# A YOCO conformer trunk on one core: the last expert pair kept on chip, a layer norm root in halves, output weights in four parts

## The reference, cut to what matters

```python
def conformer_conv(h, w_in, b_in, w_dw, b_dw, ln_g, ln_b, w_out, b_out):
    a, gate = jnp.split(h @ w_in + b_in, 2, axis=-1)
    u = a * jax.nn.sigmoid(gate)
    u = lax.conv_general_dilated(u, w_dw[:, None, :], ...) + b_dw
    u = jax.nn.silu(layer_norm(u, ln_g, ln_b))
    return u @ w_out + b_out

def hierarchical_moe(h, r_grp, r_exp, w_gate, w_up, w_down):
    ...
    hid = jax.nn.silu(a) * u * gates[:, :, None]
    y = jnp.einsum("tef,efd->td", hid, w_down)

x = x + conformer_conv(rms_norm(x, a_norm), ...)
x = x + hierarchical_moe(rms_norm(x, ffn_norm[0]), ...)
kv = shared_kv(x, kv_norm, w_kv)
x = x + dilated_attention(rms_norm(x, b_norm), ..., kv)
x = x + hierarchical_moe(rms_norm(x, ffn_norm[1]), ...)
out = rms_norm(x, final_norm)
```

## Time and profile before

| | |
|---|---|
| median of 3 runs | 1626.92 us (1626.81 to 1626.94) |
| the profiled execution's own time | 1628.82 us |
| its span, first to last instruction | 1627.0 us |
| mean granted clock of PE | 0.966 of full speed |
| busy: PE / DVE / ACT / POOL | 1517.0 / 1052.5 / 672.4 / 388.2 us |
| chain that ended last | PE 74%, DVE 12%, DMA 9%, ACT 3% of the span |

### The profile page before, as it was taken

How to read it: one execution, slowest core, us unless ns; L and a number is a source line. 1 busy time by engine, 2 the same in 40 slices (tenths; PEclk the granted TensorE clock), 3 DMA queues, 4 the chain that set the end, 5 groups by cost and what they waited for, 6 DMA issues and landing times.

```text
span 1627.0 us, 19661 instructions
## 1 busy us (share of the span) xinstructions
PE 1517.0 (93%) x7236; PEld 1172.2 (72%) x7236; DVE 1052.5 (65%) x1284; ACT 672.4 (41%) x730; POOL 388.2 (24%) x341
## 2 busy tenths in 40 slices
PE   6999798999999967999999999999999799999992
PEld 5887485766666735888888888888888576766661
DVE  6995728555656529775857777686872865555554
ACT  5111635455555515324233232423243555555542
POOL 3000012222222214332405142240501222222120
PEclk9999798999999987999999999999999899999996
DMA  5223507788888836212112121211336468888854
GB/s 204 78 74 117 219 39 286 306 339 339 338 344 341 332 125 231 83 54 75 64 52 90 39 83 59 77 60 56 120 148 239 173 282 356 347 360 340 346 233 168
DMA packets 52358, 309.83 MB, mean 190 GB/s; under 512 B 10336, under 2 KB 16096, under 8 KB 38496
## 3 DMA queue, kind: packets, MB, share of 16 engines
q1 hardware_dynamic: 41808, 291.28, 45.6%
q0 software_dynamic: 9648, 16.80, 2.9%
q10 hardware_dynamic: 864, 1.26, 0.2%
HBM read 299.33 MB, written 28.31 MB: 201 GB/s over the span
## 4 chain that ended last, share of the span: by engine, by line
PE 74%; DVE 12%; DMA 9%; ACT 3%; issue 2%; SPq 0%; DVEq 0%; POOL 0%; ACTq 0%; POOLq 0%
PE PS L1774 11%; PE PS L1837 5%; PE PS L1839 5%; PE PS L1838 5%; DMA WR<-w_up 5%; DVE taps_sb L1104 4%; PE PS L1922 3%; PE PS L1938 3%; PE PS L1753 3%; PE PS L1749 3%; PE PS L1750 3%; PE PS L1736 3%; PE PS L1734 3%; PE PS L1735 3%; PE PS L1853 3%; PE PS L1855 3%
## 5 line engine op out<-in xcount | busy, mean ns | idle before, releaser
L1375 DVE TENSOR_TENSOR wgl<-WR,wgh 128x2048 fp32r<-128x2048 f32 x66 | 148.6, 2290 | 213.9 <-ACT wgh L882 212.8
L728 POOL TENSOR_TENSOR KQ<-rope_ab 64x512 f32<-64x512 f32 x96 | 173.7, 1809 | 364.7 <-DVE rope_ab L1464 361.1
L1774 PE MATMUL PS<-WR,SC 128*128 128x512 f32 x528 | 234.9, 598 | 3.1 <-ACT SC L919 1.7
L1774 PEld LDWEIGHTS PS<-WR,SC 128*128 128x128 f32 x528 | 99.4, 191 | 118.3 <-issue 116.2
L951 ACT ACTIVATE wh<-wraw 128x1024 fp32r<-128x1024 f32 x76 | 80.3, 1057 | 249.5 <-PE PS L1839 248.7
L1375 DVE TENSOR_TENSOR wul<-WR,wuh 128x2048 fp32r<-128x2048 f32 x66 | 148.0, 2284 | 0.9 <-ACT wuh L882 0.9
L882 ACT ACTIVATE wgh<-WR 128x2048 fp32r<-128x2048 f32 x66 | 122.4, 1905 | 60.1 <-DMA WR<-w_gate 60.1
L882 ACT ACTIVATE wuh<-WR 128x2048 fp32r<-128x2048 f32 x66 | 122.6, 1905 | 31.1 <-PE PS L1736 19.5
L1464 DVE TENSOR_TENSOR rope_ab<-PS,rope_sb 32x512 f32<-32x512 f32 x192 | 131.9, 687 | 2.6
L1749 PE MATMUL PS<-wgh,xgh 128*128 128x512 f32 x264 | 110.8, 420 | 2.5 <-DVE wgl L1375 2.5
L1446 DVE TENSOR_TENSOR wl<-wraw,wh 128x1024 fp32r<-128x1024 f32 x76 | 93.1, 1225 | 28.0 <-ACT wh L951 26.3
(11 more groups left out here) (286 smaller groups left out, 3284.4 us busy)
## 6 DMA issues: line engine op xcount, KB each, us to landing
WR<-w_gate SPq DMA_DIRECT2D x33, 2048.0 KB, 15.5
WR<-w_up SPq DMA_DIRECT2D x33, 2048.0 KB, 16.7
WR<-w_down SPq DMA_DIRECT2D x33, 2048.0 KB, 9.0
wraw<-w_qkv SPq DMA_DIRECT2D x72, 512.0 KB, 3.3
WR<-w_in SPq DMA_DIRECT2D x8, 1024.0 KB, 4.9
WO<-w_out SPq DMA_DIRECT2D x2, 2048.0 KB, 8.0
xn_dram<-SC SPq DMA_DIRECT2D x8, 512.0 KB, 2.9
HT<-y_dram SPq DMA_DIRECT2D x8, 512.0 KB, 6.6
```

The source lines that it names most:

```text
L728: nc.gpsimd.tensor_tensor(to, cos, sin, ALU.add).then_inc(rope_done, 1)
L1375: V.tensor_tensor(lo[:, kts, :], raw[:, kts, :], hi[:, kts, :].bitcast(F32), ALU.subtract).then_inc(done, 1)
L1774: ins = M.matmul(PS[3 + h][:, :], hidT[:, ft, :], wd[b][:, ft, h * 512:(h + 1) * 512], start=ft == 0, stop=ft == FT - 1)
```

## The change

1. **Start.** ACT's `y_done` copies, and the wait for the constants ahead of them, go behind the four roots.
2. **Taps.** DVE takes 3 taps of chunk 0 before `gated(1)` instead of 9, and the others after it.
3. **Output weights.** `w_out` comes in four transfers of 1 MB, at other places of SP's queue, each further forward.
4. **Mean.** DVE adds chunks 0 to 5 up ahead; PE multiplies that sum, chunk 6, and, by 16 products of 128x128 with a matrix `onesp`, chunk 7 as it lies in phases in `yph[0]`, before its way through DRAM.
5. **Root.** ACT reads the variance from PSUM with EPS as bias; root, reciprocal, the first product, silu and rounding of chunk 0 go in two halves of the tokens; the tables of Sqrt and Silu are loaded ahead by dummy operations; PE starts chunk 0 with its 16 hi products, the 8 lo ones follow. `wo_lead` 5 to 7 go between the silu of chunks 1 to 3.
6. **Last pair.** Its rows are not scattered. POOL stores zeros to their places in `y_dram` at the start of the layer (`clear`), SP loads `y_dram` while the last pair is computed, and DVE adds these rows (`add_stored`, the eight operations of `combined`) then. DVE builds a 128 x 512 matrix of mixing weights for each block of the last pair (`place_last`), PE transposes it, and PE sums its rows (`sum_rows`: 8 products of 512 columns for each expert) straight into PSUM; DVE adds them to X (`add_last`).
7. **Around it.** The hidden tile of the last pair is copied by ACT, not DVE. PE transposes the rows of "kv" once all four quarters of X are there. SP issues the first loads of `w_qkv` before the last pair ends, and `rope` after the stores of `x_dram`.

```diff
 out_of_phases(1)
 win_load(7)
+sp.dma_start(WE, a["w_out"][:, 0:2, :]).then_inc(wout_in[0], 16)
 out_of_phases(3)
+sp.dma_start(WO[:, 6:KT, :], a["w_out"][:, 6:KT, :]).then_inc(wout_in[1], 16)
 into_phases(5)
 into_phases(6)
 out_of_phases(5)
 into_phases(7)
 sp.wait_ge(u_mm, KT)
-sp.wait_ge(taps_done, len(BY_TAPS))
-sp.dma_start(WO[:, 0:KT // 2, :], a["w_out"][:, 0:KT // 2, :]).then_inc(wout_in[0], 16)
+sp.dma_start(WO[:, 2:4, :], a["w_out"][:, 2:4, :]).then_inc(wout_in[0], 16)
 out_of_phases(6)
 out_of_phases(7)
-sp.wait_ge(conv_in[0], (len(BY_BANDS) + 1) // 2 * PH * 16)
-sp.dma_start(WO[:, KT // 2:, :], a["w_out"][:, KT // 2:, :]).then_inc(wout_in[1], 16)
+sp.wait_ge(taps_done, len(BY_TAPS))
+sp.dma_start(WO[:, 4:6, :], a["w_out"][:, 4:6, :]).then_inc(wout_in[1], 16)
...
-    sp.wait_ge(y_stored[l][0], (last + 1) * 16)
-    sp.wait_ge(y_stored[l][1], seconds)
+    for b in range(2):
+        sp.wait_ge(y_stored[l][b], last * 16)
+    sp.wait_ge(y_cleared.sem, y_cleared.at(32 * (l + 1)))
     for n in range(NT):
+        if n == 2:
+            sp.wait_ge(gate_mm[l], 2 * last + two + 1)
         for k in range(2):
-            sp.dma_start(yg[k][:, n, :], y_dram[l][k * T + n * P:k * T + (n + 1) * P, :]).then_inc(x_in[n], 16)
...
+last_0 = moe_sp(0)
+sp.wait_ge(up_mm[0], 2 * last_0 + 1)
...
+    def clear(b):
+        nc.gpsimd.tensor_copy(zcol[b], slot_ids[:, bass.ds(2 * last + b, 1)]).then_inc(p_steps, 1)
+        steps.n += 1
+        steps.wait()
+        nc.gpsimd.tensor_tensor(idle[:, :], ident[:, 0:1], ident[:, 0:1], ALU.mult)
+        pool.indirect_dma_start(y_dram[l], bass.IndirectOffsetOnAxis(ap=zcol[b], axis=0), zeros, None,
+                                bounds_check=2 * T - 1, oob_is_err=False).then_inc(y_cleared.sem, 16)
...
+    for b in range(2):
+        clear(b)
-    scatter(0, last)
-    with pool.If(two > 0):
-        scatter(1, last)
...
+        act.wait_ge(const_in, 48)
+        for c, s in enumerate(y_done):
+            nc.scalar.activation(spare[:, 4 + c:5 + c], ident[:, 0:1], ACT.Copy).then_inc(s, 1)
...
+nc.scalar.activation(spare[:, 13:14], eps, ACT.Sqrt)
...
 wo_lead(4)
-wo_lead(5)
-act.wait_ge(ln_d, KT + 1)
-nc.scalar.activation(lnstd, lnstd, ACT.Sqrt).then_inc(ln_sq, 1)
-wo_lead(6)
-wo_lead(7)
-for c in range(KT):
-    act.wait_ge(ln_n, c + 1)
-    nc.scalar.activation(SL[:, c, :].rearrange("p (t s) -> p s t", s=PH), HTQ[:, c, :].rearrange("p (s t) -> p s t", s=PH),
+act.wait_ge(var_mm, KT)
+for ts in HALVES:
+    nc.scalar.activation(turned(lnstd)[:, :, ts], turned(PS[5][:, :])[:, :, ts], ACT.Sqrt, bias=eps).then_inc(ln_sq, 1)
+nc.scalar.activation(spare[:, 14:15], eps, ACT.Silu)
+def silu(c, m, ts):
+    act.wait_ge(ln_n, m)
+    nc.scalar.activation(in_phases(SL[:, c, :])[:, :, ts], turned(HTQ[:, c, :])[:, :, ts],
                          ACT.Silu, bias=cv[:, C_LNB + c:C_LNB + c + 1],
                          scale=cv[:, C_LNG + c:C_LNG + c + 1]).then_inc(silu_done, 1)
+    act.wait_ge(silu_done, m)
+    nc.scalar.activation(HTh[:, c, tok], SL[:, c, tok], ACT.Copy).then_inc(silu_lead, 1)
+for m, ts in enumerate(HALVES):
+    silu(0, m + 1, ts)
+for c in range(1, KT):
+    silu(c, c + 2, slice(0, TP))
+    if c < 4:
+        wo_lead(4 + c)
...
+            def copy_hidT(b):
+                act.wait_ge(hT_mm[l], 2 * i + (b + 1))
+                if b == 1:
+                    act.wait_ge(down_mm[l], 2 * i + 1)
+                nc.scalar.activation(hidT.rearrange("p a b -> p (a b)"), PS[2][:, :], ACT.Copy).then_inc(hidT_done[l], 1)
             with act.If(two > 0):
                 gate_lead(1, i + 1, 2 * i + 1)
                 up_lead(1, i + 1, 2 * i + 1)
                 silu_gate(1)
+            copy_hidT(0)
+            act.wait_ge(spread_mm.sem, spread_mm.at(l + 1))
+            nc.scalar.activation(spread_w[0], PS[5][:, :], ACT.Copy).then_inc(spread_sb.sem, 1)
             store_y(0)
             with act.If(two > 0):
+                copy_hidT(1)
+                act.wait_ge(y_done[l], 2 * i + 2)
+                nc.scalar.activation(yst[1], yst[0], ACT.Copy)
+                nc.scalar.activation(spread_w[1], PS[5][:, :], ACT.Copy).then_inc(hidT_done[l], 1)
+                act.wait_ge(hidT_done[l], 2 * i + 3)
+                nc.scalar.activation(spread_w[0], PS[6][:, :], ACT.Copy)
                 store_y(1)
...
-taps(0, 0, 9)
+taps(0, 0, 3)
 gated(1)
-taps(0, 9, 12)
+taps(0, 3, 12)
...
 biased(6)
+for b in range(2):
+    dve.wait_ge(conv_in[b], (2 - b) * PH * 16)
+steps.mark(V.tensor_tensor(lnstd, HTQ[:, 0, :], HTQ[:, 1, :], ALU.add))
+for c in range(2, 6):
+    steps.wait()
+    steps.mark(V.tensor_tensor(lnstd, lnstd, HTQ[:, c, :], ALU.add))
+presum_done.append(steps.n)
 biased(7)
 dve.wait_ge(mean_mm, 1)
-for b in range(2):
-    dve.wait_ge(conv_in[b], (len(BY_BANDS) + 1 - b) // 2 * PH * 16)
 for c in range(KT):
+    if c >= KT - 2:
+        dve.wait_ge(conv_in[KT - 1 - c], (2 + (c == KT - 1)) * PH * 16)
...
     wo_trail(c)
-dve.wait_ge(var_mm, KT)
-V.tensor_scalar(lnstd, PS[5][:, :], EPS, None, ALU.add).then_inc(ln_d, 1)
-dve.wait_ge(ln_sq, KT + 1)
-steps.step(V.reciprocal(lnstd, lnstd))
+wol_done.append(steps.n)
 dve.wait_ge(ln_d, KT)
-for c in range(KT + 2):
+for m, ts in enumerate(HALVES):
+    root, first = turned(lnstd)[:, :, ts], turned(HTQ[:, 0, :])[:, :, ts]
+    dve.wait_ge(ln_sq, KT + m + 1)
+    steps.step(V.reciprocal(root, root))
+    V.tensor_tensor(first, first, root, ALU.mult).then_inc(ln_n, 1)
+for c in range(1, KT + 2):
     if c < KT:
         V.tensor_tensor(HTQ[:, c, :], HTQ[:, c, :], lnstd, ALU.mult).then_inc(ln_n, 1)
     if c >= 2:
         if c - 2 >= KT // 2:
             wo_trail(c - 2)
-        dve.wait_ge(silu_lead, c - 1)
+        dve.wait_ge(silu_lead, c)
         V.tensor_tensor(HTl[:, c - 2, :], SL[:, c - 2, :], HTh[:, c - 2, :].bitcast(F32), ALU.subtract).then_inc(silu_trail, 1)
...
-def combined(n, l):
+def add_stored(n, l):
     dve.wait_ge(x_in[n], 48 * (l + 1))
-    steps.step(V.scalar_tensor_tensor(X[:, n, :], yg[0][:, n, :], wt[0][:, n, :], X[:, n, :], ALU.mult, ALU.add))
-    V.scalar_tensor_tensor(X[:, n, :], yg[1][:, n, :], wt[1][:, n, :], X[:, n, :], ALU.mult, ALU.add).then_inc(x_upd.sem, 1)
+    steps.step(V.scalar_tensor_tensor(X[:, n, :], yq[n][0], wt[0][:, n, :], X[:, n, :], ALU.mult, ALU.add))
+    V.scalar_tensor_tensor(X[:, n, :], yq[n][1], wt[1][:, n, :], X[:, n, :], ALU.mult, ALU.add).then_inc(y_added.sem, 1)
+def add_sum(n, h):
+    cols = slice(h * 512, (h + 1) * 512)
+    return V.tensor_tensor(X[:, n, cols], X[:, n, cols], PS[SUM_BANKS[(2 * n + h) % 4]][:, :], ALU.add)
+def add_last(n, l, two):
+    if n == 0:
+        dve.wait_ge(sum_add[l].sem, 2 * NT * two + sum_add[l].at(0))
+    for h in range(2):
+        dve.wait_ge(sum_mm[l].sem, 2 * NT * two + sum_mm[l].at(2 * n + h + 1))
+        ins = add_sum(n, h)
+    ins.then_inc(x_upd.sem, 1)
...
+        steps.step(V.scalar_tensor_tensor(mix[b], col, last2[:, b:b + 1], wt_all, ALU.is_equal, ALU.mult))
+        steps.mark(V.tensor_tensor(to, rk_hot[:, 0:NT, :], over_rows(mix[b][:, 0:NT]), ALU.mult))
+        steps.step(V.tensor_tensor(part, rk_hot[:, NT:, :], over_rows(mix[b][:, NT:]), ALU.mult))
+        if b == 0:
+            steps.step(V.tensor_tensor(to, to, part, ALU.add))
+        else:
+            V.tensor_tensor(to, to, part, ALU.add).then_inc(spread_set.sem, 1)
...
+            steps.wait()
+            for b in range(2):
+                place_last(b)
-            copy_hidT(0)
+                hidden(1)
+            for n in range(NT):
+                add_stored(n, l)
+            dve.wait_ge(y_added.sem, y_added.at((l + 1) * NT))
             with dve.If(two > 0):
-                hidden(1)
-                copy_hidT(1)
+                for n in range(NT):
+                    for h in range(2):
+                        dve.wait_ge(sum_mm[l].sem, sum_mm[l].at(2 * n + h + 1))
+                        add_sum(n, h).then_inc(sum_add[l].sem, 1)
...
+    if k == "kv":
+        pe.wait_ge(x_upd.sem, x_upd.at(k, NT))
...
+    if l == 0:
+        for n in range(NT):
+            pe.wait_ge(silu_lead, n // 2 + 1)
+            if n == 0:
+                pe.wait_ge(v_steps, wol_done[0])
+            for h in range(2):
+                hi, _ = rows(0, slice(n * P, (n + 1) * P))
+                wh_c, wl_c = weights(0, slice(h * 512, (h + 1) * 512))
+                M.matmul(PS[2 * n + h][:, :], hi, wh_c, start=True, stop=False)
+                M.matmul(PS[2 * n + h][:, :], hi, wl_c, start=False, stop=False)
+        tile_ready(0)
+        for n in range(NT):
+            for h in range(2):
+                _, lo = rows(0, slice(n * P, (n + 1) * P))
+                wh_c, _ = weights(0, slice(h * 512, (h + 1) * 512))
+                ins = M.matmul(PS[2 * n + h][:, :], lo, wh_c, start=False, stop=False)
+        row_used(ins)
+    for c in range(0 if l else 1, half):
...
-order = (0, 1, 2, 3, 5, 4, 6, 7)
-for c in order:
-    if c in BY_TAPS:
```

(37 more changed lines are left out.)

84 lines of the change are left out of this document (57 added, 27 removed).

## The result

The changed kernel takes 1598.51 us (median of 4 runs, 1596.6 to 1601.56) against 1626.93 (4 runs, 1626.81 to 1628.97): 28.4 us less, a ratio of 0.9818 with a 95% interval of 0.9807 to 0.983. Run again in another call it took 1595.70 (5 runs, 1594.42 to 1597.4) against 1627.83, 32.1 less, 0.9807 (0.9793 to 0.9822). All nine runs together have a median of 1597.04; 1597 was forecast, with a range of 1590 to 1608. Within one call its runs span 3 to 5 us, those of before 2 to 6, so it does not scatter more.

What follows compares the result with a forecast made beforehand. PE is busy for 93% of the span, so only its waits can gain or lose: 1.2 - 1.7 + 6.5 + 2.5 + 5.9 + 11.3 + 4.3 = 30.0 off 1626.9 gives 1597 us, range 1590 to 1608.

Steps and rivals of the forecast that it cites:

- Start: Kernel start: ACT's squares no longer wait for constants, copies start 1.7 us earlier, 0.5 goes back at gated(1); gain 1.2 us.
- Output weights: Convolution 5: the WO[6:8] load queued ahead of u_dram(5) makes u land late; loss 1.7 us, bounds 0 and 2.9.
- Mean: Layer norm: centring starts 5.5 us after convolution 7 instead of 12.05; gain 6.5 us, bounds 5.0 and 6.7.
- Rival D: Centring still waits for chunk 7 from DRAM and the halves run one after the other: 1606 us; chance 0.06.
- Variance: Layer norm: PE, busy with the mean right ahead, takes 9.3 us instead of 11.8 from centring; gain 2.5 us.
- Root and first chunk: Variance to end of the projection's first chunk: halves and hi products first take 10.5 us instead of 16.4; gain 5.9.
- B: Low-clock rival: PE's new short bursts stay at the low level in variance, first chunk, sums and turns: 1608 us; chance 0.18.
- Layer 0's end: After down in layer 0: PSUM sums replace scatter, load and add, turned rows copied at 613.1, not 624.39; gain 11.3 us.
- Layer 1's end: After the last down in layer 1: both experts' sums and last scaling finish earlier; gain 4.3 us, bounds 3 and 5.3.
- Nothing: place_last, zero rows and POOL's clear lie in idle time or beside loops where PE has its weights; no cost.
- C: Transfers in the way: zero rows or earlier weights push first gate weights by 2.5 us a layer: 1602 us; chance 0.10.
- E: Slower: sums wait for the adds and PE stays at the low level, 2.6 us a product: 1638 us; chance 0.04.

Runs made afterwards that it cites:

- wout_old: Changed kernel, but w_out comes in two 2 MB transfers at their old queue places, the mean staying new; 1602.92 us.
- mean_old: Changed kernel, but PE sums the eight chunks one by one as they return from DRAM, as before; 1600.01 us.
- pair_old: Changed kernel, but with parts 6 and 7 taken back: last expert pair scattered, loaded and added after the down product as before; 1615.07 us.
- zero_twice: Changed kernel, but the zero rows of the last pair are stored twice per layer, POOL waiting for the first 1 MB; 1600.59 us.
- wo_late: Changed kernel, but the load of w_out columns 6 and 7 goes out behind convolution 5's result instead of ahead of its input; 1594.47 us.
- taps_old: Changed kernel, but DVE takes nine taps of chunk 0 before gated(1), as before the change; 1597.29 us.
- start_old: Changed kernel, but ACT's y_done copies and the wait for the constants stand ahead of the four roots again; 1598.44 us.
- warm: Changed kernel plus unread PE products, 10 ahead of convolution 3 and 18 between the variance and the projection's first chunk; 1593.96 us.

## Why the prediction was right, step by step

The measured 28.4 and 32.1 lie around the 30.0 of the sum, but not every term is right: layer 0's end brought 3.1 more than its term, the start 0.7 more, and 1.3 came unforeseen, while the root and the first chunk brought 0.8 to 1.8 less and the convolutions lost 0.7 to 1.2 more. That the sum fits is in part luck, since these cancel.

- *Start*, forecast 1.2, came 1.9. The half microsecond that I took off for the sigmoid did not appear, since the sigmoid came forward with the start too (it ends at 41.54), and DVE reaches `gated(1)` only at 43.10: the first fused tap is itself 2.90 long (40.28).
- *Output weights*, forecast -1.7, came -2.9 and -2.4, and only in part for the reason given. The load ahead of `u_dram(5)` did stretch it (3.1 to 5.7 over all profiles that have it there, 2.0 in the others), but PE waited 1.52 for it in the first execution and not at all in the second. What both have is the slow convolution 3 (1.6), which I had not seen: PE now comes earlier and waits longer for it. In the second execution its u was also written in 3.8 instead of 2.0. So the size of the term is luck there. Where convolution 3 is fast, the same load costs about 3 at convolution 5 (wout_old against mean_old, pair_old and zero_twice). And the gain of the new places, 4.5, I had put to the mean.
- *Mean*, 6.5 came as 6.5, but as 4.5 from the weights' places and 2.0 from the mean (mean_old, wout_old). The step that failed is "centring starts at 163.30: 12.05 us, with `c_dram` in the chain": I had the 8.10 us of the earlier trace rows in hand as the price of 2 MB in the queue, used it for the loss at convolution 5, and did not ask what its removal gives. Rival D's 6.5 for the mean would for the same reason have been 2.0. In the working, 2 x 0.89 and 16 x 0.24 are 5.6 before any handover, not 5.5; it came 5.3.
- *Variance*, 2.5, came 2.7, by two errors that cancel: the sum has some 4 us at the low level, and the granted clock was 1.00 throughout; and it has 7.1 for the eight products, which took 7.7. Nor does it need the new mean right ahead of it: mean_old has the same 7.7.
- *Root and first chunk*, 5.9, came 5.4 less 1.3 or 0.3. PE started 4.2 after the end of the variance, not 3.75, and the chunk took 8.3 and 7.3, not 6.7, since twelve and eight records ran low, not six: there B was right in part. The new load of the Silu table starts at 167.83, takes 1.28, and the dummy behind it starts at 169.13; the drain of 1380 ns that the Trainium skill ("ScalarE: Activation LUTs", What ACT_TABLE_LOAD costs) adds is not there either, and the 1.4 that I had estimated from it did not come.
- *Layer 0's end*, 11.3, came 14.4. The fourth quarter of X was there 8.8 after the sums' start (PE's turning starts at 593.17, the sums at 584.33), as worked out. The turning was sized too high: 3.79 for all 32 turns, so `HQh` starts 3.3 behind the fourth quarter, not 4.6; and the sums start 1.8 sooner, since `down` runs at the full level, 7.11 instead of 8.80. In the changed kernel the new transposes stand ahead of it where PE used to wait.
- *Layer 1's end*, 4.3, came 4.4 and 4.7.
- *Nothing*: the loops kept their time, but for the 1.0 of new transposes in that of layer 1. The table load of Silu lay beside the reciprocals, as said. 1.3 more came on the way into layer 0's experts, unforeseen; twelve of the thirteen profiles with the change have it (58.0 to 58.8 from first add to first silu), pair_old (58.2) among them, so it is not the last pair's. Only one profile of before stands against them (59.5), and its cause stays open.

Two readings of the trace before were off. From convolution 7 to the first product of the projection PE is idle for 14.5 of 33.2 us, not for most of 40. And PE does not fall to the low level after each pause: ahead of convolutions 1 and 3 it waits 1.62 and 1.02 us, and both run at a granted clock of 1.00.

B's other places (variance, sums) did not come. C came in part, at u: the Trainium skill ("DMA: Bandwidth & Descriptors", Issuing engines are not separate DMA queues) has transfers of all engines end on the same DMA engines. The weights ahead of u did hold it up, though both stand in one engine's queue here; the zero rows, which POOL issues beside SP's loads, cost 0.8 at most. D fell: centring came 5.3 after convolution 7 in both executions. E fell: a sum costs 0.89, and adds run beside it.

## What to carry to other kernels

Ask of each transfer that a change moves who stands behind it in the queue at its old place too: removing 2 MB from ahead of a 256 KB result gave more up to centring (4.5) than the new arithmetic that was built to avoid waiting for it (2.0). Two parts of a change can share a gain or need each other: here the new mean brought nothing up to centring alone, and either part brought the whole gain of the variance, so test both cells before crediting one. One profile is one execution: that of wo_late showed no price of the load ahead of u, and three others, compared with wout_old, showed about 3 us. And count where an engine will idle after a gain upstream: PE came earlier, idled, and gave 1.6 of it back in a convolution at a granted clock of 0.83.

## What the runs showed of the hardware

Convolution 3, 72 records, takes 8.30 us at a granted clock of 1.00 after a wait of 1.02, 1.08, 1.34, 1.56 or 1.60 us, 9.93 or 9.94 at 0.83 after 2.46, 3.20, 3.56 or 3.63, and 10.85 at 0.75 after 3.91; with unread products ahead of it it takes 8.20 to 8.30 at 1.00. The length of the wait alone does not decide it: convolution 5 took 9.93 at 0.83 after 2.80 us (taps_old) and 8.30 at 1.00 after 2.85 (pair_old), and ahead of the turning of the rows 2.05 us left the 32 turns at 3.83 in one execution (start_old) and 5.45 in another (warm).

A 256 KB write of u issued 0.7 to 2.5 us behind a 1 MB load in SP's queue landed 0.63 to 0.65 us after that load in all nine profiles that have the two in this order, and so took 3.1 to 5.7; the write of `c_dram(6)` behind 2 MB landed 0.68 (before) and 0.64 (wout_old) after them. The write of `u_dram(3)`, 256 KB, with no weights just ahead of it in SP's queue, took from 2.0 to 4.1 us from execution to execution. With the clock behind it, the end of convolution 3 lies anywhere from 92.4 to 95.5 us in the six profiles that don't differ ahead of it.
